# First two weight units loaded and split by halves of their input channels, interleaved with the input's halves

## The reference, cut to what matters

```python
def first_block(x, norm_mix, w_in, ...):
    u = rms_norm(h, norm_mix[l])                 # h is x at first
    proj = u @ w_in[l]                           # 1024 x 2568
    pool_out = pool_mixer(proj[..., :P], ...)
    qkv = causal_conv_silu(proj[..., P:P + 3 * G], conv_w[l])
    z = proj[..., P + 3 * G:P + 4 * G]
    a = proj[..., P + 4 * G:P + 4 * G + H]       # the last 8 columns of w_in
    b = proj[..., P + 4 * G + H:P + 4 * G + 2 * H]
    gdn_out = gated_delta_net(...)               # l2 norms of q, k; decays from a; a triangular solve
```

## Time and profile before

| what | value |
|---|---|
| median of three runs | 1064.49 us |
| the profiled execution's own time | 1063.67 us |
| its span | 1061.9 us |
| TensorE busy (matmul) | 1041.2 us, 98% |
| VectorE, ScalarE busy | 711.8 us, 540.7 us |
| the chain that ended last, by engine | PE 84%, DVE 10%, ACT 3%, issue 2% |
| HBM read | 165.03 MB, 156 GB/s over the span |

### The profile page before, as it was taken

How to read it: one execution, slowest core, us unless ns; L and a number is a source line. 1 busy time by engine, 2 the same in 40 slices (tenths; PEclk the granted TensorE clock), 3 DMA queues, 4 the chain that set the end, 5 groups by cost and what they waited for, 6 DMA issues and landing times.

```text
span 1061.9 us, 21149 instructions
## 1 busy us (share of the span) xinstructions
PE 1041.2 (98%) x8986; PEld 1010.1 (95%) x8986; DVE 711.8 (67%) x987; ACT 540.7 (51%) x651; POOL 33.1 (3%) x39
## 2 busy tenths in 40 slices
PE   8999999999999999999999999999999999999997
PEld 7999999999997899999999999998898999999997
DVE  6889665455567777666556567699978666555463
ACT  7947653434446465354444447796553254443431
POOL 0004000000000000000000000032000000000000
PEclk9999999999999999999999999999999999999999
DMA  9622475556745656555555544414100157555511
GB/s 295 216 81 81 159 263 174 197 163 212 267 149 158 202 170 212 163 168 202 195 162 194 198 158 119 139 65 153 63 2 2 48 181 255 192 180 175 197 40 40
DMA packets 119042, 167.02 MB, mean 157 GB/s; under 512 B 5824, under 2 KB 99648, under 8 KB 118592
## 3 DMA queue, kind: packets, MB, share of 16 engines
q1 hardware_dynamic: 117792, 165.92, 47.8%
q10 hardware_dynamic: 1184, 0.17, 0.1%
HBM read 165.03 MB, written 1.05 MB: 156 GB/s over the span
## 4 chain that ended last, share of the span: by engine, by line
PE 84%; DVE 10%; ACT 3%; issue 2%; DMA 0%; POOL 0%; DVEq 0%; ACTq 0%; POOLq 0%
PE banks L2038 25%; PE banks L2039 24%; PE banks L2040 24%; DVE sb_w_low L1231 1%; DVE sb_arena L1876 1%; DVE sb_state L1873 1%; PE banks L2593 1%; PE banks L2473 1%; PE banks L2130 1%; ACT sb_w_high L656 0%; DMA sb_x<-in_x_t 0%; PE banks L2704 0%; DVE sb_arena L1390 0%; DVE sb_state L1387 0%; PE banks L2579 0%
## 5 line engine op out<-in xcount | busy, mean ns | idle before, releaser
L1231 DVE TENSOR_TENSOR sb_w_low<-sb_raw,sb_w_high 128x2048 fp32r<-128x2048 f32 x148 | 338.1, 2290 | 242.6 <-ACT sb_w_high L656 242.6
L656 ACT ACTIVATE sb_w_high<-sb_raw 128x2048 fp32r<-128x2048 f32 x148 | 281.9, 1911 | 262.5 <-PE banks L2040 261.7
L2038 PE MATMUL banks<-sb_act_high,sb_w_low 128*128 128x256 f32 x1368 | 391.7, 286 | 1.3 <-POOL sb_act_low L634 0.5
L2040 PE MATMUL banks<-sb_act_high,sb_w_high 128*128 128x256 f32 x1368 | 387.1, 283 | 0.0
L2039 PE MATMUL banks<-sb_act_low,sb_w_high 128*128 128x256 f32 x1368 | 385.5, 282 | 0.0
L2038 PEld LDWEIGHTS banks<-sb_act_high,sb_w_low 128*128 128x128 f32 x1368 | 258.3, 189 | 4.7 <-POOL sb_act_low L634 2.4
L2039 PEld LDWEIGHTS banks<-sb_act_low,sb_w_high 128*128 128x128 f32 x1368 | 258.7, 189 | 0.5 <-issue 0.2
L2040 PEld LDWEIGHTS banks<-sb_act_high,sb_w_high 128*128 128x128 f32 x1368 | 256.8, 188 | 0.0
L2038 PE MATMUL banks<-sb_hidden_high,sb_w_low 128*128 128x256 f32 x896 | 253.5, 283 | 0.6 <-DVE sb_hidden_low L1699 0.6
L2040 PE MATMUL banks<-sb_hidden_high,sb_w_high 128*128 128x256 f32 x896 | 253.7, 283 | 0.0
L2039 PE MATMUL banks<-sb_hidden_low,sb_w_high 128*128 128x256 f32 x896 | 253.0, 282 | 0.0
(11 more groups left out here) (426 smaller groups left out, 1033.8 us busy)
## 6 DMA issues: line engine op xcount, KB each, us to landing
sb_raw<-in_ffn_w SPq DMA_DIRECT2D x64, 1024.0 KB, 5.3
sb_raw<-in_w_up SPq DMA_DIRECT2D x16, 1024.0 KB, 5.4
sb_raw<-in_w_down SPq DMA_DIRECT2D x16, 1024.0 KB, 5.0
sb_raw<-in_sgu_w_in SPq DMA_DIRECT2D x16, 1024.0 KB, 5.3
sb_raw<-in_rwkv_w_rkv SPq DMA_DIRECT2D x12, 1024.0 KB, 5.6
sb_raw<-in_w_in SPq DMA_DIRECT2D x8, 1024.0 KB, 9.6
sb_raw<-in_sgu_w_out SPq DMA_DIRECT2D x8, 1024.0 KB, 5.0
sb_raw<-in_w_out SPq DMA_DIRECT2D x4, 1024.0 KB, 5.2
```

What stands on the lines that cost most here:

```text
L656: nc.scalar.activation(whi[s][:], raw[s][:], ACT.Copy).then_inc(hi_done, 1)
L1231: nc.vector.tensor_tensor(wlo[s][:], raw[s][:], f32(whi[s][:]), ALU.subtract).then_inc(lo_done, 1)
L2038: nc.tensor.matmul(dst, l_lo, r_hi, start=start, stop=False, **kw)
L2040: return nc.tensor.matmul(dst, l_hi, r_hi, start=False, stop=stop, **kw)
```

## The change

Units 0 and 1 are halved along the input channels (k 0 to 3 and k 4 to 7, all 256 output columns) in place of the output columns. SP's order becomes x half 0, unit 0 half 0, x half 1, unit 0 half 1, then the halves of unit 1. ScalarE and VectorE split four tiles of x, then a half of unit 0, and so twice; both squares of x move behind the halves of unit 1 on ScalarE, and the folding moves behind the low halves of unit 1 on VectorE; the load of the a/b weights is issued behind half 1 of unit 0; `high(2)` moves ahead of the scale, and `low(2)` ahead of `take_pre(0)` (behind the wait for the scale). TensorE's `first` takes four channel tiles at a time into both column halves of its bank, and `input_squares()` stands between the halves of unit 1. The unread products are 16 of ones by ones, 128 columns, that wait for no input.

```diff
-    half_of = lambda w, t: w[:, :].rearrange("p (k n) -> p k n", k=KT)[:, :, t * P:t * P + P]
+    half_of = lambda w, h: w[:, :].rearrange("p (k n) -> p k n", k=KT)[:, 4 * h:4 * h + 4, :]
...
+        def load_half(j, h):
+            c = IN_COLS[j]
+            sp.dma_start(half_of(raw[j], h), w_in_v[:, 4 * h:4 * h + 4, c * 256:c * 256 + 256])\
+                .then_inc(landed[j] if h else half_landed[j], 16)
+
         for h in range(2):
             sp.dma_start(x[:, 4 * h:4 * h + 4, :],
                          dram["x_t"].rearrange("(k p) t -> p k t", p=P)[:, 4 * h:4 * h + 4, :]).then_inc(x_in[h], 16)
+            load_half(0, h)
         for j, c in enumerate(IN_COLS):
-            if j < 2:
-                for t in range(2):
-                    sp.dma_start(half_of(raw[j], t), w_in_v[:, :, c * 256 + t * P:c * 256 + t * P + P])\
-                        .then_inc(landed[j] if t else half_landed[j], 16)
-            else:
+            if j == 1:
+                for h in range(2):
+                    load_half(1, h)
+            if j > 1:
                 inner(U_IN + j, w_in_v, c)
...
-        high_half(0, 0)
+        for h in range(2):
+            for k in range(4 * h, 4 * h + 4):
+                input_high(k)
+            high_half(0, h)
         act.dma_start(MX.wab[:], by_k(dram["w_in"][0])[:, :, IN_WIDTH - 8:IN_WIDTH]).then_inc(ab_in, 16)
-        x_squares(0)
-        high_half(0, 1)
-        x_squares(1)
         high_half(1, 0)
         high_half(1, 1)
+        x_squares(0)
+        x_squares(1)
         act.wait_ge(ab_in, 16)
         nc.scalar.activation(wab_hi[:], MX.wab[:], ACT.Copy).then_inc(ab_col, 1)
+        high(2)
         act.wait_ge(ss_done, 1)
         act.wait_ge(const_set, 1)
         rsqrt_of_sums(MX.rB, bank[7][:, 0:T], D).then_inc(r_done, 1)
...
-        high(2)
         first_tap(0)
...
-        low_half(0, 0)
-        low_half(0, 1)
+        for h in range(2):
+            for k in range(4 * h, 4 * h + 4):
+                input_low(k)
+            low_half(0, h)
+        low_half(1, 0)
+        low_half(1, 1)
         dve.wait_ge(x_squared, 2)
         chain.add(nc.vector.tensor_tensor(MX.sq[:, 0:4, :], MX.sq[:, 0:4, :], MX.sq[:, 4:8, :], ALU.add))
         chain.settle()
         nc.vector.tensor_tensor(MX.sq[:, 0:2, :], MX.sq[:, 0:2, :], MX.sq[:, 2:4, :], ALU.add).then_inc(sq_done, 1)
-        low_half(1, 0)
-        low_half(1, 1)
...
         dve.wait_ge(r_done, 1)
         dve.wait_ge(edges_set, 1)
+        low(2)
         take_pre(0)
-        low(2)
         taps(0)
...
+        def first(j, ks):
+            w_hi, w_lo = (w[j][:, :].rearrange("p (k n) -> p k n", k=KT) for w in (whi, wlo))
+            h = ks[0] // 4
+            tiles = [(k, t, slice(t * P, t * P + P), bank[j][:, t * T:t * T + T]) for k in ks for t in range(2)]
+            if j == 0:
+                pe.wait_ge(hi_done if h else hi_half, 1)
+                for k, t, cs, dst in tiles:
+                    pe.wait_ge(a_lo, A_MIX + k + 1)
+                    nc.tensor.matmul(dst, w_hi[:, k, cs], act_hi[:, k, :], start=k == 0 and t == 0, stop=False,
+                                     skip_group_check=True)
+                    nc.tensor.matmul(dst, w_hi[:, k, cs], act_lo[:, k, :], start=False, stop=False, skip_group_check=True)
+                pe.wait_ge(lo_done if h else lo_half, 1)
+                for k, t, cs, dst in tiles:
+                    ins = nc.tensor.matmul(dst, w_lo[:, k, cs], act_hi[:, k, :], start=False, stop=k == KT - 1,
+                                           skip_group_check=True)
+            else:
+                pe.wait_ge(lo_done if h else lo_half, j + 1)
+                for k, t, cs, dst in tiles:
+                    ins = split_matmul(dst, w_hi[:, k, cs], w_lo[:, k, cs], act_hi[:, k, :], act_lo[:, k, :],
+                                       start=k == 0 and t == 0, stop=k == KT - 1, skip_group_check=True)
+            if h:
+                ins.then_inc(w_used, 1)
...
         pe.wait_ge(const_set, 1)
-        pe.wait_ge(x_in[0], 16)
-        for _ in range(6):
-            nc.tensor.matmul(bank[7][:, 0:T], ones, x[:, 0, :], start=True, stop=True)
-        first(0)
+        for _ in range(16):
+            nc.tensor.matmul(bank[7][:, 0:P], ones, ones, start=True, stop=True)
+        first(0, range(0, 4))
+        first(0, range(4, 8))
+        first(1, range(0, 4))
         input_squares()
-        first(1)
+        first(1, range(4, 8))
```

More of the change, by code:

```diff
@@ L672, in _, with input_high, high_half @@
         act.wait_ge(vec_in, 16)
-        for k in range(KT):
+        def input_high(k):
             act.wait_ge(x_in[k // 4], 16)
             nc.scalar.activation(act_hi[:, k, :], x[:, k, :], ACT.Copy, scale=vcol("norm_mix", k)).then_inc(a_hi, 1)
-        def high_half(j, t):
-            act.wait_ge(landed[j] if t else half_landed[j], 16)
-            nc.scalar.activation(half_of(whi[j], t), half_of(raw[j], t), ACT.Copy).then_inc(hi_done if t else hi_half, 1)
+        def high_half(j, h):
+            act.wait_ge(landed[j] if h else half_landed[j], 16)
+            nc.scalar.activation(half_of(whi[j], h), half_of(raw[j], h), ACT.Copy).then_inc(hi_done if h else hi_half, 1)
         def x_squares(h):
@@ L1242, in _, with input_low @@
         nc.vector.tensor_tensor(SG.g[:], vcol("norm_final", 0, 8), vcol("norm_mix_g0", 0, 8), ALU.mult).then_inc(g_done, 1)
-        for k in range(KT):
+        def input_low(k):
             dve.wait_ge(x_in[k // 4], 16)
@@ L1247, in _, with low_half @@
                                            ALU.mult, ALU.subtract).then_inc(a_lo, 1)
[L1249 to L1252, removed]
-        low_half(0, 0)
-        low_half(0, 1)
+        def low_half(j, h):
+            dve.wait_ge(hi_done if h else hi_half, j + 1)
+            nc.vector.tensor_tensor(half_of(wlo[j], h), half_of(raw[j], h), half_of(f32(whi[j][:]), h), ALU.subtract)\
+                .then_inc(lo_done if h else lo_half, 1)
+        for h in range(2):
[4 more added lines that the diff above has]
+        low_half(1, 1)
         dve.wait_ge(x_squared, 2)
@@ L2099, in part @@
             quarter(U_IN + j, j % 2, n)
[L2101 to L2119, removed]
```

## The result

The changed kernel takes 1070.62 us (median of 4 runs, 1069.65 to 1071.84) against 1064.37 before: 1.0058 of it, 95% interval 1.0045 to 1.007. It is 6.25 us slower, where 2.1 were forecast; the profiled execution took 1070.72 us with a span of 1068.9, 7.0 us above the span before. The mean granted clock of the four runs was 0.993 to 0.995. One run of the experiments, e3's at 1442.29 us with a mean granted clock of 0.649, was slow throughout and is left out of every comparison.

The account below looks back on a forecast made before the run. After norms(1), ScalarE's and VectorE's lists were taken to bound the kernel: first_tap(1) 2.36 us later, less 0.22 of slack, gave 2.14 us and 1066.6 us against the median; range 1063.9 to 1067.9.

Parts of the forecast that it names:

- What bounds the kernel: TensorE paces until norms(1) at 34.17 us, then ScalarE and VectorE until L2202; ScalarE has only 0.22 us to spare.
- Rival (c): Head of the kernel: TensorE's earlier start is kept, chain 2 us shorter, 1062.5 us; chance 0.10.
- TensorE's start: Unread products through by about 8.4 us; first product with weights at 7.9 us in place of about 10.6.
- The loads: Halves in 1 KB rows move faster; last half of unit 1 lands at 12.7 us, units 2 and 3 about 1.3 earlier.
- The squares: Squares move behind unit 1 on ScalarE, folded by VectorE at 17.64 us; by them r_done would be 19.66.
- rival (a): The squares decide r_done, not the a/b weights: 1.4 us later, 1065.9 us; chance 0.32.
- The a/b weights: Their later-issued load holds ScalarE's list: landing at 17.46 us, r_done 20.39 in place of 18.41.
- I take 7.7, from the same load: Assumed the a/b load again takes 7.7 us from issue to landing, so it lands at 17.46.
- The bound from above, 18.5: Latest a/b landing, with unit 2's 3.0 us ahead less 2 us of earlier draining; r_done 21.4.
- Rival (b): The a/b weights land at 18.5 us or later, behind unit 2 and the constants; 3.1 us later, 1067.6; chance 0.13.
- TensorE doesn't come later than ScalarE: At norms(1): TensorE, after waiting for silu(0) to 28.7, ends near 34.2 us, before the scales due at 36.3.
- Rival (d): At the start the clock stays low until 11 us, making r_done 20.9 and the time 1067.1 us; chance 0.05.

Follow-up runs that it names:

- e3: Changed kernel with high(2) again behind the scale and low(2) again behind take_pre(0), a/b load still late; median 1067.78 us, ratio 1.0034.
- e5: Changed kernel with the a/b load ahead of unit 2 and unread products in TensorE's two remaining waits; median 1065.65 us, ratio 1.0021.
- e6: Changed kernel with the a/b load ahead of unit 2 and low(2) ahead of VectorE's wait for the scale; median 1063.56 us, ratio 0.9994.
- e1: Changed kernel with the a/b load issued by SyncE ahead of unit 2; median 1068.55 us, ratio 1.0041.
- e2: Changed kernel with unread products of ones in TensorE's waits to hold the clock; median 1068.84 us, ratio 1.0046.
- e8: Changed kernel with a/b load ahead of unit 2, squares in ScalarE's gaps, and reordered ScalarE and VectorE lists; median 1062.57 us, ratio 0.9989.
- e9: Changed kernel with the a/b load issued by ScalarE behind the first half of unit 0; one run, 1065.84 us beside 1064.13 before.
- e7: Kernel before with only the new unread products, 16 of ones by ones waiting for no input; median 1064.97 us, ratio 1.0008.

## Why the prediction was wrong

**What bounds the kernel: right.** The chain passes norms(1) and then belongs to ScalarE and VectorE to L2202; first_tap(1) late by d makes the end late by d less 0.22. In e5 (first_tap(1) + 2.12, span + 1.9), e6 (+ 0.24, - 0.2) and the changed kernel with its clock held (+ 5.62, + 5.1) this holds to 0.3 us. Rival (c) was rightly put low: TensorE's first product came 1.6 us earlier (8.50 for 10.13) and nothing of it was kept, and in e6, where nothing else was late, TensorE was 1.15 us earlier at norms(1) and the inversion only 0.03.

**TensorE's start.** First product at 8.50, not 7.9, since the first half of x landed 0.6 us later (5.79 for 5.19); no cost. The unread products were through at 6.34 where 8.4 was reckoned, and between 7.2 and 7.8 in e1, e2, e5 to e8.

**The loads: right.** 1 KB rows moved at 346 to 350 GB/s; half 1 of unit 1 was there at 13.2 for 12.7, with the same 0.6 us behind it.

**The squares: right where they could be seen.** In e1, where they decide, r_done comes at 20.6 for the 19.66 of rival (a), of which 0.7 stand already at the last half of unit 1 (13.44 for 12.74), and first_tap(1) at 28.78 for 27.87; the step between them is again 8.2.

**The a/b weights: this term was mis-sized, and it is the larger part of the miss.** The step "I take 7.7, from the same load" gave a landing at 17.46; it was 20.77, 0.48 us from the later issue and 2.8 from a delay of 10.5. The bound from above, 18.5, was too low as well: it priced unit 2's bytes ahead of the load, while the load's packets, from 14.2 on, went one for one with the larger ones of the constants and with unit 3's. r_done came at 23.66 for 20.39, 3.27 later, and the 3.3 us pass to the end undiminished, since the step from r_done to first_tap(1) measured 8.18 for the 8.21 forecast. Rival (b), 1067.6 at a chance of 0.13, was the nearest: it had the late load deciding, but standing behind unit 2 and the constants, and at too low a price.

**Sum, "TensorE doesn't come later than ScalarE": this step failed.** It put norms(1) near 34.2 with a wait for silu(0) in it, and did not ask what those waits do to the clock. With the late scale there were 4.7 us of waits between 25 and 32, the clock fell to 0.50, and TensorE came to norms(1) 1.48 us after ScalarE. Rival (d) had the clock, but at the start, where it behaved: the unread products were through at 6.34, and the clock was still up at 8.50.

Together 2.14 + 3.27 + 1.48 = 6.9 of the 7.0 us of span. The last two terms aren't independent: it was the late load that gave TensorE its waits, and e1, which moved only the load, won back 4.6 us with most of the wait for norms(1). The same by the experiments' profiled spans: 1068.9 less 1.9 for the clock (e2, 1067.0), less 3.2 for the load (e5, 1063.8), less 2.1 for low(2) (e6, 1061.7), against 1061.9 before.

The Trainium skill's rule on the round between queues ("DMA: Bandwidth & Descriptors", Queues, rings and completion order) gave an early landing, and no run has it: each of the four issues from ScalarE waited 3.7 us or more for its first packet. Once packets moved, though, they did alternate with SyncE's (from 17 to 18.5 us of the changed kernel, 416 of the one and 416 of the other queue), as the rule has it.

## What to carry to other kernels

Where a filler engine is busy at 98% and a chain on other engines sets the pace, first find how far ahead each in-order list is at the handover (0.22 us here), and price a change by what stands behind each wait in that list: a small load behind which a list waits belongs ahead of the large ones, and work that is ready belongs before a wait, not behind it. Measure the landing of a small-row DMA at its new place rather than carrying its old delay over. And count the waits that a delay gives to TensorE: 4.7 us of them between 25 and 32 us cost it the clock here, which 21 unread products kept up. With smaller waits it went either way: TensorE had 1.03 and 0.65 us of them in e1's profile and in e9's, with the same busy time, and the clock fell in the first (0.81 from 28 to 31) and stayed at 1.00 in the second.

## What the runs showed of the hardware

- Runs of one kernel lay 3 us apart, in seven of the eight kernels of the table and in the one before too (30 runs at 1063.3 to 1065.5, five at 1066.4 to 1068.0), with a mean granted clock of about 0.995 in the longer. The profiled execution of e3 shows a place: after a stretch of small matmuls (32 and 64 rows) with a wait of 0.7 us, the clock goes to 0.50, far from anything that was edited. Its windows:

```profile
822.00:824.00 2.00, 1.32 (x23) 1.18 (x22) 1.93 (x4) 0.59 (x1) 0.00 (x0) 1.00 0.03 8
824.00:826.00 2.00, 2.00 (x23) 1.93 (x22) 2.00 (x5) 0.36 (x1) 0.00 (x0) 0.96 0.00 0
826.00:828.00 2.00, 2.00 (x11) 2.00 (x11) 1.93 (x4) 0.84 (x3) 0.00 (x0) 0.50 0.00 0
828.00:830.00 2.00, 2.00 (x12) 1.87 (x10) 0.50 (x2) 0.16 (x1) 0.00 (x0) 0.69 0.00 0
```

  The profile of e7 has it too (0.66 over 820 to 830), the other nine have not, although the changed kernel has the same 1.32 us of busy time in a window there (826 to 828) at a clock of 1.00. In e7 the inversion's first product stands at 62.48, 1.30 after that of the kernel before, and the span is 4.2 above it: 2.9 us were lost behind it, and no other window of 10 us from 20 us on is below 1.00. For e7 this place makes the 3 us; for the runs without a profile that isn't shown, and why the clock falls there in some executions stays open.
- The kernel before spread over 2.2 us even in its 30 runs at the higher clock, e6 over 0.4 us in its eight. In the profile of before, high(3) waits 0.79 us for unit 3, and in that of e7 1.66; in e6's it doesn't wait. That this is the reason for the spread wasn't tested.
- A load of 1024 rows of 32 bytes took 7.6 to 10.8 us from issue to landing over all profiles, in which, at 348 GB/s, 2.6 to 3.8 MB pass in rows of 1 KB.
